# Attention layer of a decoder trunk: projection pieces ahead of the sparse products, one piece divided round the compressed scores, stick-breaking sums and scores interleaved

## The chip, the cores and the metric

One core of one Trainium2 chip runs the whole program. The metric is the device time of one execution in microseconds; lower is better. Of the before kernel three executions were timed, and one further execution was profiled. All times of rows below are from that profiled execution, in microseconds from the start of its span unless marked ns.

## What is computed

A trunk of two layers over 256 rows of width 1024, in float32. Layer 0 has the mixer that the change touches, layer 1 a gated recurrence; each is followed by a mixture of 32 experts of which a row uses two. The expert weights are read from memory once each.

```python
h = x
for layer in range(2):
    hn = rms_norm(h, norm_mix[layer])
    mix = nsa_stickbreak_mixer(hn, ...) if layer % 2 == 0 else hgrn2_mixer(hn, ...)
    h = h + mix
    h = h + hier_moe(rms_norm(h, norm_ffn[layer]), ...)
return rms_norm(h, final_norm)

# nsa_stickbreak_mixer
q_a, k_c, v_c, k_s, v_s, k_w, v_w, gate, q_b, k_b, v_b = split(h @ w_in)
o_cmp, sel_idx, sel_ok = nsa_compressed_and_select(q_a, compress(k_c), compress(v_c))   # 15 compressed blocks
o_sel, o_win = nsa_selected_and_window(q_a, k_s, v_s, k_w, v_w, sel_idx, sel_ok)        # softmax per branch
o_a = gate[0] * o_cmp + gate[1] * o_sel + gate[2] * o_win                              # 8 heads
# stick breaking, 8 heads
z = q_b @ k_b.T * scale
log_keep = where(before, log_sigmoid(-z), 0)
later = cumsum(log_keep, reverse=True) - log_keep
o_b = where(before, exp(log_sigmoid(z) + later), 0) @ v_b
return concatenate([o_a, o_b]) @ w_out
```

## The kernel before, in words

Five engines run instruction streams of their own, in the order in which the code writes them, and wait for each other by counting semaphores. Where an instruction waits, all that is behind it on its engine waits too. The change is in layer 0's attention, and there in TensorE's, ScalarE's and VectorE's order.

**Projections.** h @ w_in is computed in 12 parts, proj(0) to proj(11), each with 8 input blocks of 128 and two halves. A product is kept near float32 by splitting both operands into a high and a low part and adding three products: high by high and high by low in one run of 16 matmuls of 128x256 (L1770 with L1774 or L1772), then low by high in 8 more (L1781 or L1779). So one half of a part, called a piece here, is 24 matmuls. ScalarE makes the high part of a weight quarter (L798), VectorE the low part (L379). The parts alternate between banks 0 and 1; ScalarE empties the even parts (proj_even), VectorE the odd ones (proj_odd), and the semaphore proj_psum counts finished parts. proj(6) and proj(7) make the stick-breaking queries, proj(8) and proj(9) the keys, proj(10) and proj(11) the values.

**Compressed branch.** TensorE multiplies the compressed keys (L1872) and values (L1874), ScalarE copies them out (L920 to L922), and then 16 small matmuls with 15 columns each (L1888, two records each in the trace) make the compressed scores. VectorE masks them, takes the maxima and subtracts (L1280 to L1285), and ScalarE takes the exponentials (L930). The first sparse scores wait for that VectorE work (semaphore cmp_step). In the before kernel the whole of proj(6) stands behind the scores.

**Sparse branches.** Eight units, u = 0 to 7, are two query tiles by two branches (selected, window) by two halves of the heads. For each unit: scores on TensorE (nsa_scores, L1902), mask and maximum on VectorE (mask, L1298, L1301), exponentials on ScalarE (exps, L941), division and gate on VectorE (scale, L1308 to L1314), transposes of the probabilities on TensorE (nsa_T, L1914), copies out of the transposes on ScalarE (L973) and, for u of 4 and more, also on VectorE (L1355), and the product with the values on TensorE (nsa_pv, L1928). In turn u TensorE issues nsa_scores(u+1), nsa_pv(u-1), the pieces of a projection that a table PROJ_AT gives to this turn (one piece in turns 0 to 3, two in turns 4 to 6, none in turn 7), and nsa_T(u). Behind a finished odd part it raises unit_used (free_units), which lets the queue on SyncE load expert weights into the place of the weights just used. Turn 7 has the stick-breaking scores sb_z(0) and sb_z(1) ahead of nsa_T(7).

**Stick breaking.** Eight heads in four pairs. sb_z(pair) makes the scores of two heads and adds the mask (L1947, L1951, L1955). VectorE turns them into a maximum and a negative absolute value (sb_abs, L1323, L1324), ScalarE takes exponential and logarithm (exp_ln, L947, L948), VectorE adds the two (L1370, semaphore sb_t), TensorE adds the running sums to the scores in the same bank (sb_e, L1962 to L1964), ScalarE takes the exponential (L988, semaphore sb_a), and TensorE multiplies with the values (sb_pv, L1977). VectorE's third buffer makes sb_abs(hd) wait for sb_e(hd-3). Heads 6 and 7 use the banks of heads 0 and 1, so sb_z(3) waits for the first two exponentials of L988. Between them the result of the sparse branches is split too: ScalarE copies two banks (L983, mix_hi) and VectorE subtracts (out_low, L1359, mix_lo); sb_pv(0) and sb_pv(2) write into these banks and wait for it. Behind it all come the products with w_out (mix_front, mix_tile).

**Queue.** SyncE issues the weight loads in a fixed order, each behind a wait: at L418 for places in the ring, at L469 for the expert weights that go where the attention's buffers were. The last of these in the attention wait for sb_pv of all heads (L1977).

## Time and profile before

| | us |
|---|---|
| three timed executions | 743.26, 746.83, 748.84 (median 746.83) |
| profiled execution, its own time | 749.39 |
| its span, first to last instruction | 747.70 |
| mean granted TensorE clock | 0.938 of full speed |
| TensorE busy | 628.5 (84% of the span) |
| VectorE busy | 307.7 (41%) |
| ScalarE busy | 242.3 (32%) |

The page gives the chain of work that ended last as 52% TensorE and 32% DMA, and within the DMA share 30% is one kind of transfer, the experts' down weights. The busy shares are means over stages that are limited by different things, so they are read by stage: the first part of the span is layer 0's attention, then come routing and the first experts of layer 0, then a long stretch with the later experts; layer 1 has its recurrence in the place of the attention and the same experts' stages behind it. 1.69 us of the execution's time lie outside the span.

### The profile page before, as it was taken

The page shows a single profiled execution, that of the slowest core. Times are in us where ns is not written, and L with a number is a line of the kernel's source. Part 1 is how long each engine was busy: PE and PEld are TensorE (multiplying, and loading weights), DVE is VectorE, ACT ScalarE, POOL GpSimd, SP SyncE. Part 2 cuts the span into 40 slices and gives each one's busy share as a digit, 9 for nine tenths or more (in the row PEclk, how much of TensorE's full clock was granted, in tenths as well). Part 3 has the DMA queues.
Part 4 walks back from the last instruction along what each step waited for, and adds up shares of the span by engine and source line. Part 5 has one row for each costly group of instructions (what it writes and reads, how often), then busy time and mean ns, then how long its engine had stood idle before and what let it go on. Part 6 is the DMA issues. An engine that isn't in the chain of part 4 may idle for free.

```text
span 747.7 us, 11876 instructions
## 1 busy us (share of the span) xinstructions
PE 628.5 (84%) x4862; PEld 435.3 (58%) x4862; DVE 307.7 (41%) x536; ACT 242.3 (32%) x546; POOL 35.9 (5%) x64
## 2 busy tenths in 40 slices
PE   7999898799998674955989999999999984595775
PEld 6987687697444322413259999999854441331321
DVE  4555677645223211202276786754432220211204
ACT  5434544525121100101156675553521110110113
POOL 5100000000001100000000001060000000000000
PEclk9998999999999977979999999999999998887979
DMA  8967333699999999999997536369989999999993
GB/s 314 257 208 286 113 113 120 250 391 343 391 406 404 403 423 420 419 421 423 411 387 273 204 135 226 124 243 369 389 341 399 414 422 422 423 420 419 422 418 146
DMA packets 59857, 245.08 MB, mean 328 GB/s; under 512 B 4560, under 2 KB 8928, under 8 KB 39072
## 3 DMA queue, kind: packets, MB, share of 16 engines
q1 hardware_dynamic: 58400, 242.33, 82.9%
q0 software_dynamic: 768, 1.40, 0.6%
q8 instruction: 34, 0.56, 0.3%
q10 hardware_dynamic: 640, 0.67, 0.3%
q14 instruction: 15, 0.12, 0.0%
HBM read 243.34 MB, written 1.05 MB: 327 GB/s over the span
## 4 chain that ended last, share of the span: by engine, by line
PE 52%; DMA 32%; DVE 5%; SPq 5%; ACT 3%; issue 2%; DVEq 0%; ACTq 0%
DMA ring<-in_moe_w_down 30%; PE psum L1770 9%; PE psum L2184 6%; PE psum L2129 6%; PE psum L1779 5%; PE psum L1772 5%; PE psum L1781 4%; PE psum L1774 4%; SPq L510 3%; PE psum L2122 3%; SPq L477 2%; DMA ring<-in_att_w_in 2%; PE psum L2113 1%; PE psum L1928 1%; PE psum L2301 1%
## 5 line engine op out<-in xcount | busy, mean ns | idle before, releaser
L2129 PE MATMUL psum<-ring,xT 128*32 128x512 f32 x512 | 66.8, 678 | 35.4 <-DMA ring<-in_moe_w_up 35.4
L1501 DVE TENSOR_TENSOR arena<-psum,arena 128x256 f32<-128x256 f32 x16 | 6.8, 425 | 214.8 <-ACT arena L1016 214.8
L2129 PE MATMUL psum<-arena,xT 128*32 128x512 f32 x512 | 65.3, 668 | 35.5 <-DMA arena<-in_moe_w_up 35.5
L1012 ACT ACTIVATE arena<-psum 128x256 f32<-128x256 f32 x16 | 6.1, 384 | 206.1 <-PE psum L2129 206.1
L2184 PE MATMUL psum<-ring,arena 128*32 128x512 f32 x456 | 58.6, 595 | 12.6 <-DMA ring<-in_moe_w_down 12.6
L1770 PE MATMUL psum<-x_hi,w_hi 128*128 128x256 f32 x248 | 63.7, 293 | 1.5 <-DVE x_hi L1188 1.2
L798 ACT ACTIVATE w_hi<-ring 128x1024 fp32r<-128x1024 f32 x48 | 48.8, 1051 | 44.2 <-PE psum L1781 21.0
L2129 PEld LDWEIGHTS psum<-arena,xT 128*32 128x32 f32 x512 | 17.0, 121 | 79.0 <-issue 42.5
L2122 PE MATMUL psum<-arena,xg 128*128 128x128 f32 x512 | 61.8, 278 | 0.8 <-DVE arena L1487 0.8
L2129 PEld LDWEIGHTS psum<-ring,xT 128*32 128x32 f32 x512 | 16.9, 123 | 77.8 <-issue 41.1
L2122 PEld LDWEIGHTS psum<-arena,xg 128*128 128x128 f32 x512 | 59.6, 194 | 2.7 <-issue 2.7
L379 DVE TENSOR_TENSOR w_lo<-ring,w_hi 128x1024 fp32r<-128x1024 f32 x44 | 52.3, 1221 | 18.4 <-ACT w_hi L798 18.4
L2113 PE MATMUL psum<-xT,arena 128*128 128x512 f32 x128 | 57.7, 594 | 0.0
L1770 PEld LDWEIGHTS psum<-x_hi,w_hi 128*128 128x128 f32 x248 | 48.9, 197 | 3.2 <-issue 1.6
L1774 PE MATMUL psum<-x_hi,w_lo 128*128 128x256 f32 x192 | 48.5, 289 | 0.0
L1483 DVE TENSOR_TENSOR h<-psum,h 128x512 f32<-128x512 f32 x64 | 44.2, 690 | 9.3 <-PE psum L2113 8.2
L2184 PEld LDWEIGHTS psum<-ring,arena 128*32 128x32 f32 x456 | 15.0, 109 | 48.8 <-issue 33.2
L1770 PE MATMUL psum<-w_hi,x_hi 128*128 128x256 f32 x160 | 39.7, 286 | 0.9 <-issue 0.8
L1772 PE MATMUL psum<-w_lo,x_hi 128*128 128x256 f32 x160 | 39.2, 283 | 0.0
L1774 PEld LDWEIGHTS psum<-x_hi,w_lo 128*128 128x128 f32 x192 | 38.0, 198 | 0.0
L2113 PEld LDWEIGHTS psum<-xT,arena 128*128 128x128 f32 x128 | 23.1, 190 | 24.6 <-issue 24.6
L1781 PE MATMUL psum<-x_lo,w_hi 128*128 128x256 f32 x248 | 35.6, 287 | 0.1
(334 smaller groups left out, 1044.1 us busy)
## 6 DMA issues: line engine op xcount, KB each, us to landing
ring<-in_moe_w_down SPq DMA_DIRECT2D x54, 1024.0 KB, 20.7
ring<-in_moe_w_gate SPq DMA_DIRECT2D x32, 1024.0 KB, 15.7
ring<-in_moe_w_up SPq DMA_DIRECT2D x32, 1024.0 KB, 17.6
arena<-in_moe_w_gate SPq DMA_DIRECT2D x32, 1024.0 KB, 21.3
arena<-in_moe_w_up SPq DMA_DIRECT2D x32, 1024.0 KB, 23.2
ring<-in_rec_w_in SPq DMA_DIRECT2D x16, 1024.0 KB, 13.9
ring<-in_att_w_in SPq DMA_DIRECT2D x8, 1024.0 KB, 11.7
ring<-in_att_w_out SPq DMA_DIRECT2D x4, 1024.0 KB, 13.5
```

What stands on the lines that cost most here:

```text
L379: eng.tensor_tensor(quarter_lo(base, r), quarter(base, r), quarter_hi(r).bitcast(F32), ALU.subtract)\
L798: act.activation(quarter_hi(r), quarter(base, r), ACT.Copy).then_inc(s["w_high"], 1)
L1483: dve.tensor_tensor(v, bank(b), v, ALU.add).then_inc(done, 1)
L1770: pe.matmul(dst, a_hi(k), b_hi(k), start=(k == 0), stop=False)
L1772: pe.matmul(dst, a_hi(k), b_lo(k), start=False, stop=False)
L1774: pe.matmul(dst, a_lo(k), b_hi(k), start=False, stop=False)
L1779: last = pe.matmul(dst, a_lo(k), b_hi(k), start=False, stop=(k == KD - 1))
L1781: last = pe.matmul(dst, a_hi(k), b_lo(k), start=False, stop=(k == KD - 1))
L2113: pe.matmul(bank(b), shareT[:, t, :], y_rows[:, half * 512:(half + 1) * 512], start=True, stop=True).then_inc(s[f"combined{l}"], 1)
L2122: last = pe.matmul(gather_bank(k, first)[:, k % 4 * P:(k % 4 + 1) * P], xg_parts[:, t, k, :], slots[:, t].rearrange("p e c -> p (e c)"), s ...
L2129: return pe.matmul(bank(3)[e * CAP:(e + 1) * CAP, :].rearrange("p (w f) -> p w f", w=2), gatheredT[:, k, e * CAP:(e + 1) * CAP], w, start= ...
L2184: last = pe.matmul(bank(5 + c)[e * CAP:(e + 1) * CAP, :], hidT[:, j, e * CAP:(e + 1) * CAP], down_part(l, kind, e, j)[:, c * 512:(c + 1) * ...
```

## The change

It moves instructions and adds none. (1) proj(6) is cut into its two pieces; the first is issued ahead of the wait for the compressed keys and values, the second stays behind the compressed scores. (2) In every turn u the projection pieces and the raising of unit_used, and in turn 7 sb_z(0) and sb_z(1), are issued ahead of the product nsa_pv(u-1). (3) In stick breaking TensorE issues sb_e(0) ahead of sb_z(2) and sb_z(3) ahead of sb_e(3). (4) ScalarE copies the two sparse banks one at a time, behind the exponentials of heads 0 and 1, where it copied both ahead of the first; VectorE's two subtractions come with heads 2 and 4, where both came with head 1.

```diff
@@ scalar, stick breaking
             for hd in range(SB_H):
                 if hd + 2 < SB_H:
                     exp_ln(hd + 2)
-                if hd == 0:
-                    act.wait_ge(s["nsa_pv"], 8)
-                    for g in range(NSA_G):
-                        act.activation(mix_hi[:, 2 * g:2 * g + 2, :], bank(6 + g).rearrange("p (a t) -> p a t", a=2),
-                                       ACT.Copy).then_inc(s["oT_high"], 1)
                 act.wait_ge(s["sb_e"], hd + 1)
                 if hd >= 3:
                     act.wait_ge(s["sb_pv"], (hd - 3) // 2 * 2 + 2)
                 act.activation(za[:, hd % 3, :], bank(SB_BANKS[hd])[:, 0:384], ACT.Exp).then_inc(s["sb_a"], 1)
+                if hd < NSA_G:
+                    act.wait_ge(s["nsa_pv"], 8)
+                    act.activation(mix_hi[:, 2 * hd:2 * hd + 2, :], bank(6 + hd).rearrange("p (a t) -> p a t", a=2),
+                                   ACT.Copy).then_inc(s["oT_high"], 1)
@@ vector, stick breaking
                 if hd + 2 < SB_H:
                     sb_abs(hd + 2)
-                if hd == 1:
-                    for g in range(NSA_G):
-                        dve.wait_ge(s["oT_high"], g + 1)
-                        dve.wait_ge(s["proj_psum"], 12)
-                        out_low(2 * g, 6 + g)
+                if hd in (2, 4):
+                    g = hd // 2 - 1
+                    dve.wait_ge(s["oT_high"], g + 1)
+                    dve.wait_ge(s["proj_psum"], 12)
+                    out_low(2 * g, 6 + g)
@@ tensor, compressed branch
             last.then_inc(s["cmp_product"], 1)
+            proj(6, (0,))
             pe.wait_ge(s["cmp_kv_done"], 3)
             pe.wait_ge(s["proj_odd"], 1)
...
             last.then_inc(s["cmp_product"], 1)
-            proj(6)
+            proj(6, (1,))
@@ tensor, sparse branches
             for u in range(8):
                 if u + 1 < 8:
                     nsa_scores(u + 1)
+                if u in PROJ_AT:
+                    proj(*PROJ_AT[u])
+                if PROJ_DONE.get(u) in (7, 9, 11):
+                    free_units(1)
+                if u == 7:
+                    sb_z(0)
+                    sb_z(1)
                 if u == 1:
...
                 if u >= 1:
                     nsa_pv(u - 1)
-                if u in PROJ_AT:
-                    proj(*PROJ_AT[u])
-                if PROJ_DONE.get(u) in (7, 9, 11):
-                    free_units(1)
                 if u == 0:
...
                     last.then_inc(s["cmp_product"], 1)
-                if u == 7:
-                    sb_z(0)
-                    sb_z(1)
                 nsa_T(u)
@@ tensor, stick breaking
+            sb_e(0)
             sb_z(2)
-            sb_e(0)
             sb_e(1)
             sb_e(2)
+            sb_z(3)
             sb_e(3)
             sb_pv(0)
-            sb_z(3)
             sb_e(4)
```

The changed code is one line shorter above TensorE's part, so that L1770 of the rows before is L1769 in the changed kernel, L1774 is L1773, L1781 is L1780, and on ScalarE L988 becomes L983 and L983 becomes L986.

**First place: TensorE round the compressed scores.** Before, the small products of keys and values (L1872, L1874) are followed at once by the scores (L1888), and then by the first matmuls of proj(6):

```order
L1872 MATMUL psum<-arena 64x30 [waits cmp_step]
L1874 MATMUL psum<-arena 128x64 x2
L1888 MATMUL psum<-arena 128x15 [waits proj_odd,cmp_kv_done]
L1888 MATMUL psum<-arena 128x15 x15
L1770 MATMUL psum<-x_hi,w_hi 128x256 [waits w_low_dve,proj_even]
L1774 MATMUL psum<-x_hi,w_lo 128x256
```

Changed, here is the end of the first piece of proj(6), the scores, and the start of the second piece:

```order
L1773 MATMUL psum<-x_hi,w_lo 128x256
L1780 MATMUL psum<-x_lo,w_hi 128x256 x8
L1888 MATMUL psum<-arena 128x15 [waits proj_odd,cmp_kv_done]
L1888 MATMUL psum<-arena 128x15 x15
L1769 MATMUL psum<-x_hi,w_hi 128x256 [waits w_low_dve]
L1773 MATMUL psum<-x_hi,w_lo 128x256
```

The 24 matmuls of one piece have moved from behind the scores to ahead of them, and with them the wait for proj_even.

**Second place: TensorE in turn 4 of the sparse branches.** Before, between the transposes of unit 3 (first two rows) and proj(9) stand the scores of unit 5 and the product of unit 3 (L1928), with its wait for the copies out of the transposes:

```order
L1914 MATMUL psum<-ident,arena 128x128 [waits nsa_pT_even,nsa_scaled]
L1914 MATMUL psum<-ident,arena 128x128 x3
L1902 MATMUL psum<-arena 128x256 [waits nsa_masked]
L1902 MATMUL psum<-arena 128x256 x3
L1928 MATMUL psum<-arena 64x128 [waits nsa_pT_even]
L1928 MATMUL psum<-arena 64x128 x3
```

Changed, that product comes behind the last 8 matmuls of proj(9), directly ahead of the transposes of unit 4:

```order
L1780 MATMUL psum<-x_lo,w_hi 128x256 x8
L1928 MATMUL psum<-arena 64x128 [waits nsa_pT_even]
L1928 MATMUL psum<-arena 64x128 x3
L1914 MATMUL psum<-ident,arena 128x128 [waits nsa_pT_even,nsa_scaled]
L1914 MATMUL psum<-ident,arena 128x128 x7
L1902 MATMUL psum<-arena 128x256 [waits nsa_masked]
L1902 MATMUL psum<-arena 128x256 x3
```

The product has moved past two pieces, 48 matmuls; in turns 1 to 3 it is one piece, in turns 5 and 6 two, in turn 7 the four heads' scores.

**Third place: stick breaking, TensorE behind nsa_pv(7).** Before, sb_z(2) (L1947 to L1955) and then the sums sb_e(0):

```order
L1947 MATMUL psum<-arena 128x256 [waits nsa_pT_odd,nsa_pT_even]
L1947 MATMUL psum<-arena 128x256
L1951 MATMUL psum<-arena 128x128 x2
L1955 MATMUL psum<-before_r,ident_r 128x2x128 [waits sb_z_raw] x2
L1962 MATMUL psum<-arena 128x256 [waits sb_t]
L1963 MATMUL psum<-arena 128x128
L1964 MATMUL psum<-arena 128x128
```

Changed, the sums of the first head, then the same scores, then the sums of the second head:

```order
L1962 MATMUL psum<-arena 128x256 [waits sb_t]
L1963 MATMUL psum<-arena 128x128
L1964 MATMUL psum<-arena 128x128
L1947 MATMUL psum<-arena 128x256 [waits nsa_pT_odd,nsa_pT_even]
L1947 MATMUL psum<-arena 128x256
L1951 MATMUL psum<-arena 128x128 x2
L1955 MATMUL psum<-before_r,ident_r 128x2x128 [waits sb_z_raw] x2
L1962 MATMUL psum<-arena 128x256 [waits sb_t]
```

The scores of heads 4 and 5 have moved past one head's sums. On VectorE, before, the two subtractions L1359 stand between sb_abs(3) and the addition for head 2:

```order
L1323 TENSOR_SCALAR arena<-psum 128x384 [waits sb_e,sb_z]
L1324 SCALAR_TENSOR_TENSOR arena<-arena,psum 128x384 [waits dve_chain]
L1359 TENSOR_TENSOR mix_lo<-psum,mix_hi 128x512 [waits proj_psum,oT_high] x2
L1370 TENSOR_TENSOR arena<-arena 128x384 [waits sb_ln]
```

Changed, from sb_abs(3) on, with the first subtraction only behind sb_abs(4):

```order
L1322 TENSOR_SCALAR arena<-psum 128x384 [waits sb_e,sb_z]
L1323 SCALAR_TENSOR_TENSOR arena<-arena,psum 128x384 [waits dve_chain]
L1369 TENSOR_TENSOR arena<-arena 128x384 [waits sb_ln]
L1322 TENSOR_SCALAR arena<-psum 128x384 [waits sb_e,sb_z]
L1323 SCALAR_TENSOR_TENSOR arena<-arena,psum 128x384 [waits dve_chain]
L1358 TENSOR_TENSOR mix_lo<-psum,mix_hi 128x512 [waits proj_psum,oT_high]
L1369 TENSOR_TENSOR arena<-arena 128x384 [waits sb_ln]
```

The addition for head 2, and with it the sums sb_e(2), no longer stand behind the subtractions.

## Rows read from the trace of the kernel before

**Rows 1.** Windows: length, busy of each engine, granted clock, DMA share, GB/s.
```profile
120.00:130.00 10.00, 7.85 (x77) 6.27 (x78) 8.68 (x15) 3.89 (x8) 0.00 (x0) 1.00 0.63 214
130.00:149.00 19.00, 15.11 (x110) 12.19 (x111) 11.30 (x21) 11.56 (x23) 0.00 (x0) 1.00 0.60 247
...
226.00:375.00 149.00, 106.64 (x732) 46.02 (x728) 30.98 (x54) 18.85 (x52) 5.86 (x9) 0.87 1.01 415
...
144.00:146.00 2.00, 2.00 (x18) 1.83 (x18) 0.55 (x2) 0.22 (x1) 0.00 (x0) 1.00 0.00 0
```

**Rows 2.** Waits of the DMA queue on SyncE, 0 to 200 us: total, times, longest.
```profile
SPq L418 <- PEq L1838: 85.2, 5, 21.3
SPq L469 <- PE psum L1977: 16.8, 1, 16.8
```

**Rows 3.** Timeline of TensorE round the compressed scores: start, us, what, [idle before <-releaser].
```profile
53.62 2.48 PE L1888 MATMUL psum<-arena 64*128 64x15 f32 x32 [0.77 <-ACT arena L922]
56.03 0.58 PE L1770 MATMUL psum<-x_hi,w_hi 128*128 128x256 f32 x1
...
64.44 0.71 PE L1902 MATMUL psum<-arena 64*128 64x128 f32 x8
...
66.60 0.39 PE L1770 MATMUL psum<-x_hi,w_hi 128*128 128x256 f32 x1
...
69.57 0.60 PE L2007 MATMUL psum<-ident,arena 128*128 128x128 f32 x4
```

**Rows 4.** Windows of L1888 alone: length, PE busy, PEld busy, clock, DMA share, GB/s.
```profile
53.60:54.80 1.20, 1.19 (x22) 1.19 (x22) 1.00 0.95 323
54.87:56.10 1.23, 1.23 (x14) 1.12 (x12) 0.50 1.05 406
```

**Rows 5.** Timeline of VectorE, last work on the compressed scores ahead of cmp_step.
```profile
57.66 0.41 DVE L1285 TENSOR_TENSOR arena<-arena 128x240 f32<-128x240 f32 x1
```

**Rows 6.** Timeline of TensorE in turns 2 to 7, transposes L1914 and products L1928.
```profile
84.41 0.66 PE L1914 MATMUL psum<-ident,arena 128*128 128x128 f32 x4
...
90.85 0.66 PE L1914 MATMUL psum<-ident,arena 128*128 128x128 f32 x4 [1.07 <-DVE arena L1314]
...
93.67 0.66 PE L1928 MATMUL psum<-arena 128*64 128x128 f32 x8 [1.10 <-ACT arena L973]
...
100.54 1.06 PE L1914 MATMUL psum<-ident,arena 128*128 128x128 f32 x8 [0.26 <-issue]
...
102.86 1.09 PE L1928 MATMUL psum<-arena 128*64 128x128 f32 x16 [0.19 <-ACT arena L973]
...
112.97 1.09 PE L1928 MATMUL psum<-arena 128*64 128x128 f32 x16 [1.13 <-ACT arena L973]
...
120.25 1.06 PE L1914 MATMUL psum<-ident,arena 128*128 128x128 f32 x8 [0.26 <-issue]
...
122.19 1.09 PE L1928 MATMUL psum<-arena 128*64 128x128 f32 x16 [0.87 <-DVE arena L1355]
```

**Rows 7.** Timeline of VectorE, the scaling L1314 of units 2 and 4.
```profile
83.66 0.69 DVE L1314 TENSOR_TENSOR arena<-arena 128x512 f32<-128x512 f32 x1
...
97.69 1.23 DVE L1314 TENSOR_TENSOR arena<-arena 128x1024 f32<-128x1024 f32 x1
```

**Rows 8.** Timeline of TensorE in stick breaking: nsa_pv(7), sb_e(2), the last sb_pv.
```profile
127.85 1.09 PE L1928 MATMUL psum<-arena 128*64 128x128 f32 x16 [0.87 <-DVE arena L1355]
...
134.21 0.70 PE L1962 MATMUL psum<-arena 128*128 128x256 f32 x2 [2.10 <-DVE arena L1370]
...
147.46 0.87 PE L1977 MATMUL psum<-arena 128*64 128x256 f32 x8 [0.65 <-ACT arena L988]
```

**Rows 9.** Timeline of VectorE in stick breaking: sb_abs(3), subtractions, sb_abs(6).
```profile
131.34 0.56 DVE L1323 TENSOR_SCALAR arena<-psum 128x384 f32<-128x384 f32 x1 [1.65 <-PE psum L1964]
...
132.41 1.28 DVE L1359 TENSOR_TENSOR mix_lo<-psum,mix_hi 128x512 fp32r<-128x512 f32 x2
...
139.00 0.56 DVE L1323 TENSOR_SCALAR arena<-psum 128x384 f32<-128x384 f32 x1 [1.80 <-PE psum L1955]
```

## The prediction, made before the changed kernel ran

> **What bounds the kernel now.** I read the windows first, to see which stage is limited by what. From 226 to 375 us the DMA share is 1.01 at 415 GB/s: there the expert weights' arrival sets the pace [rows 1]. One could conclude that work on attention is worth nothing. The reader should look at two more things. From 144 to 146 us, at the end of attention, the DMA moved nothing at all [rows 1]. And the waits of the DMA queue name their releasers: 85.2 us in five waits for TensorE to free ring places, and 16.8 us for the last stick-breaking product [rows 2]. So the queue's stream of expert weights starts anew from an event in attention, and the weights that set the pace later are issued behind it. Whatever attention saves up to the last sb_pv, the whole rest of the program saves, DMA stage included. That is the exchange rate I use: 1 us for 1 us.
>
> Then I read TensorE's timeline through attention. It has three kinds of loss: a stretch at half clock round the compressed scores [rows 3, 4], waits ahead of the sparse products and transposes [rows 6], and waits in stick breaking [rows 8]. The change aims at all three, and each has another answer.
>
> **Part 1, the divided piece.** The scores start at 53.62 after a wait of 0.77, so TensorE is free at 52.85 [rows 3]. Three amounts can be won.
>
> First the wait: the piece fills it, 0.77.
>
> Second, the scores themselves. In the trace the clock falls inside them, from 2.4 to 1.2 GHz, at about 54.8, after TensorE had done little: small products, the wait, and matmuls of 15 columns. Before the fall 22 records take 1.20 us, 55 ns each; after it 14 take 1.23 [rows 4]. All 32 at the full clock take 32 x 0.055 = 1.75 us against 2.48: 0.73.
>
> Third, proj(6). Its two pieces last from 56.03 to 64.44, 8.41 us [rows 3]. A piece at the full clock, the one from 66.60 to 69.57, takes 2.97 [rows 3]; two take 5.94. So 2.47 are lost to the clock. Beside this the Trainium skill, page "TensorE: Matmul & The Clock Gate", section "Back-to-back issue gap", gives N / 2.4 + 2.5 ns for a matmul of N columns, 109 ns here. By it a piece would take 2.6 us and the loss would be 3.2; the row, 124 ns a matmul, decides.
>
> Whether the second and third amount come back depends on the clock. In the changed order a dense piece stands directly ahead of the scores, the quiet stretch shrinks from 3.25 us (52.85 to 56.10) to 1.75, and dense work follows. In 130 to 149 us TensorE is idle for 3.9 of 19 us, once for 2.10 at a stretch, and the clock stays at full speed [rows 1, 8]. I take the likelier case: no fall. Bounds are 0.77 (everything as slow as before) and 3.97.
>
> What is late now: the scores end at 52.85 + 2.97 + 1.75 = 57.57, that is 1.47 later than before. VectorE's softmax work ended 1.97 after the scores' end (57.66 + 0.41 against 56.10) [rows 3, 5], so it ends at 59.54. The second piece ends at 60.54. nsa_scores(0), which waits for that work, has 1.0 us of cover. The first sparse scores start at 60.5 instead of 64.44. **Gain 3.97.**
>
> **Part 2, pieces ahead of the sparse products.** Each nsa_pv that waited for ScalarE's or VectorE's copies now finds them done, because 3 to 6 us of projection stand ahead. But a wait that goes matters only where the following transposes are not held by VectorE. So I go through the turns.
>
> Turns 2 and 3: the transposes at 84.41 follow VectorE's scaling, which ends at 83.66 + 0.69 = 84.35 [rows 6, 7], and those at 90.85 waited 1.07 for it [rows 6]. The chain there is transposes, scores, mask, low parts of weights, scaling, transposes; TensorE's product is not in it. The changed order leaves that chain as it is, and TensorE waits at L1914 for what it did not wait at L1928. Nothing, bounds 0 and 1.
>
> Turn 4: the wait of 1.10 at 93.67 goes. VectorE's scaling ended at 97.69 + 1.23 = 98.92, the transposes came at 100.54 [rows 6, 7]: 1.62 of slack, more than 1.10. Turn 5: 0.19 at 102.86 goes, turn 6: 1.13 at 112.97 [rows 6]; they have the same two pieces and the same VectorE work, so the same slack. Sum 1.10 + 0.19 + 1.13 = 2.42, and I take it whole, since the three turns are alike.
>
> Turn 7: the wait of 0.87 at 122.19 goes too [rows 6], but from the transposes of unit 6 (120.25) on, VectorE sets the pace: it copies, makes a low part, scales and goes on with sb_abs(0) and sb_abs(1) without a pause (VectorE is busy 8.68 of 10 us [rows 1]). Its last copy of transposes comes behind these, and nsa_pv(7) waits for it. Nothing. **Gain 2.4**, bounds 1.1 and 3.3.
>
> The moved steps that others hang on: free_units now comes ahead of the product, so expert weights are issued up to 1 us earlier relative to the turn; the DMA share of 0.60 leaves room [rows 1].
>
> **Part 3, stick breaking.** From nsa_pv(7) at 127.85 to the last sb_pv at 147.46 it lasts 19.6 us [rows 8] for eight heads. VectorE has three operations of 0.56 per head (13.4 us in all) and is idle in two long waits: 1.65 for sb_e(0), which stood behind sb_z(2), and 1.80 for sb_z(3), which stood behind sb_e(3) and sb_pv(0) [rows 9]. Both orders are turned round. TensorE's wait of 2.10 at 134.21 [rows 8] is the first of these together with the subtractions of 1.28 us that stood ahead of the addition for head 2 [rows 9]. The subtractions stay in VectorE's total, so moving them wins nothing by itself; it lets ScalarE and TensorE start. If both waits went entirely, 3.45 would be won. New ones come: sb_e(1) now stands behind sb_z(2), and sb_abs(4) waits for it; sb_e(3) stands behind sb_z(3), which waits for ScalarE's exponential of head 1, and behind that sit sb_pv(0), ScalarE's head 3 and VectorE's sb_abs(6). From the lengths in the rows I put the first at 0.6 and the second, covered by sb_e(2), at nothing. **Gain 2.85**, bounds 1.3 (half of it becomes another wait) and 3.45.
>
> **Sum.** 3.97 + 2.42 + 2.85 = 9.24. The profiled execution would be 749.39 - 9.2 = 740.2. It lies 2.6 above the median of the timed runs; the same saving from the median of 746.83 gives **737.6 us**, 1.2% less. From no change a measurement of this kernel can tell about 1%, 7.5 us.
>
> **Rivals.**
>
> *The clock falls all the same.* Matmuls of 15 columns were what TensorE did when it fell, and they are still there in one block. If both pieces run as slowly as before, the first part wins 0.77 only, and the sum is 0.77 + 2.42 + 2.85 = 6.0: 740.8 us. For it: the fall came inside these very matmuls [rows 4]. Against: dense work is now on both sides of them. Chance 0.13.
>
> *The waits only change their place.* In turns 4 to 6 VectorE turns out to hold the transposes, and in stick breaking the new orders make as long waits as the old. Then part 1 stays and part 3 wins its lower bound: 4.0 + 0 + 1.3 = 5.3, 741.5 us. For it: turns 2 and 3 are of this kind already [rows 6, 7]. Against: 1.62 us of slack in turn 4. Chance 0.12.
>
> *The DMA stage takes the gain back.* If the later weights did not shift with attention, nothing would be seen: 746.8 us. Against: the empty DMA at 144 to 146 and the queue's named waits [rows 1, 2]. Chance 0.06.
>
> *Slower: half clock in stick breaking.* With its filler moved away, TensorE waits behind nsa_T(7) for VectorE's last copy, about 1.5 us, and then has small matmuls and short waits only. If that lowers the clock, the 15.11 busy us of 130 to 149 [rows 1] become 30.2, which is 11.2 more than the stretch of 19, and part 3 is lost: +11.2 - 6.4 = +4.8, 751.6 us. It becomes slower than before once some 60% of the stretch runs at 1.2 GHz. For it: the clock has fallen after quiet work once in this stage. Against: the present stretch has longer idle times and keeps its clock [rows 1, 8]. Chance 0.04.
>
> **How the numbers follow.** The forecast has 0.65. Its own range comes from the bounds that I hold possible together, gain 7 to 10, with the spread of the timed runs (743.26 to 748.84) on top: 734.5 to 741. The first two rivals lie at 740.8 and 741.5; taking them in with half their spread gives 734 to 742.5, and outside are the last two rivals and the tails, under 0.2. Faster by over 1%, below 739.4: nine tenths of 0.65 and a quarter of the first rival, 0.63. Slower by over 1% is most of the slower rival, 0.04. The rest, 0.33, is within 1%.
>
> **What the profile after would show.** Right: L1888 without a wait and in under 2 us, the clock at full speed from 50 to 65 us, nsa_scores(0) near 60.5; no waits at L1928 in turns 4 to 6, and in turns 2 and 3 a wait of about 1 us at L1914; transposes of unit 6 near 113.9; the last sb_pv near 138.2 and the queue's L469 loads right behind it; the stage of 226 to 375 unchanged in length. Wrong: a clock of 0.50 anywhere from 54 to 64 or from 118 to 138; waits at L1914 in turns 4 to 6; VectorE idle for more than 1 us between sb_abs operations; a last sb_pv that is 9 us earlier while the end of layer 0 is not.

## The result, and the profile after

The changed kernel takes 738.74 us, the median of four executions (736.00 to 741.19); four of the kernel before, measured beside it, took 743.26 to 748.84 with a median of 747.27. The ratio is 0.9892, 95% interval 0.9862 to 0.9922: a gain of 8 us, between 5.8 and 10.3. The forecast was 737.6. The profiled execution of the changed kernel has a span of 739.5 against 747.70, 8.2 less.

TensorE's timeline of the changed kernel through attention (start, us, what, idle before and releaser), to be held against [rows 3, 6, 8]:

```profile
51.73 0.66 PE L1873 MATMUL psum<-arena 128*128 128x64 f32 x4
...
55.23 1.96 PE L1888 MATMUL psum<-arena 64*128 64x15 f32 x32
...
60.19 0.49 PE L1902 MATMUL psum<-arena 64*128 64x128 f32 x4
...
79.98 0.65 PE L1914 MATMUL psum<-ident,arena 128*128 128x128 f32 x4 [1.14 <-DVE arena L1313]
...
86.43 0.66 PE L1914 MATMUL psum<-ident,arena 128*128 128x128 f32 x4 [1.07 <-DVE arena L1313]
...
94.78 0.98 PE L1914 MATMUL psum<-ident,arena 128*128 128x128 f32 x7
...
113.23 0.98 PE L1914 MATMUL psum<-ident,arena 128*128 128x128 f32 x7
...
120.58 1.09 PE L1928 MATMUL psum<-arena 128*64 128x128 f32 x16 [1.40 <-DVE arena L1354]
...
137.82 0.87 PE L1977 MATMUL psum<-arena 128*64 128x256 f32 x8 [0.65 <-ACT arena L983]
```

And four rows of the kernel before that were not shown yet, the compressed values, nsa_pv(1) in turn 2, and the first two experts' products:

```profile
52.19 0.66 PE L1874 MATMUL psum<-arena 128*128 128x64 f32 x4
...
80.63 0.66 PE L1928 MATMUL psum<-arena 128*64 128x128 f32 x8 [1.01 <-ACT arena L973]
...
181.88 2.02 PE L2122 MATMUL psum<-arena,xg 128*128 128x128 f32 x16 [0.42 <-DVE arena L1487]
...
185.68 1.05 PE L2122 MATMUL psum<-arena,xg 128*128 128x128 f32 x7
```

The last sb_pv starts at 137.82 instead of 147.46, 9.64 earlier. But the compressed values already start 0.46 earlier (51.73 against 52.19), ahead of everything that was changed. So starts are not compared below, only distances. By them the attention won 9.18, in four pieces:

| from, to | before | after | won | forecast |
|---|---|---|---|---|
| compressed values, nsa_scores(0) | 12.25 | 8.46 | 3.79 | 3.97 |
| nsa_scores(0), transposes of unit 6 | 55.81 | 53.04 | 2.77 | 2.42 |
| transposes of unit 6, nsa_pv(7) | 7.60 | 7.35 | 0.25 | 0 |
| nsa_pv(7), last sb_pv | 19.61 | 17.24 | 2.37 | 2.85 |

VectorE in stick breaking has two waits left. sb_abs(3) waits 0.43 for sb_e(0), where it waited 1.65 [rows 9], and sb_abs(4) has a new wait of 0.68 for sb_e(1). The 1.80 ahead of sb_abs(6), for sb_z(3), is gone:

```profile
122.86 0.56 DVE L1322 TENSOR_SCALAR arena<-psum 128x384 f32<-128x384 f32 x1 [0.43 <-PE psum L1964]
...
125.15 0.56 DVE L1322 TENSOR_SCALAR arena<-psum 128x384 f32<-128x384 f32 x1 [0.68 <-PE psum L1964]
```

Windows of the changed kernel (columns as in [rows 1]): the compressed scores, stick breaking, the start of the experts, and the long stage with the later experts:

```profile
50.00:65.00 15.00, 14.08 (x135) 13.21 (x134) 10.00 (x26) 5.67 (x18) 0.00 (x0) 1.00 0.86 310
118.00:138.00 20.00, 17.13 (x134) 13.75 (x132) 14.99 (x29) 13.38 (x28) 0.00 (x0) 1.00 0.64 256
174.00:177.00 3.00, 3.00 (x17) 1.27 (x20) 1.22 (x8) 0.74 (x3) 0.00 (x0) 0.53 0.51 202
218.00:366.00 148.00, 109.17 (x728) 46.39 (x728) 30.98 (x54) 18.84 (x52) 5.88 (x9) 0.86 1.01 415
```

The clock stays at full speed in both places where a rival had it fall. But it reads 0.53 at 174 to 177, while the kernel before kept 1.00 at the same place of the program (184 to 187 there). What that cost stands in TensorE's rows there:

```profile
172.26 2.71 PE L2122 MATMUL psum<-arena,xg 128*128 128x128 f32 x16 [0.42 <-DVE arena L1486]
...
177.68 0.49 PE L2122 MATMUL psum<-arena,xg 128*128 128x128 f32 x2
```

From the last sb_pv to the first expert product it is 34.44 (before 34.42), to the second 39.86 (before 38.22): 1.64 more, of which 1.62 lie between the two products. So 1.6 us of the attention's gain was lost again behind it. Queue and stage then follow one for one: the loads L477 that were issued at 226.31 before are issued at 218.31, 8.00 earlier, which is 9.64 less 1.64. From these loads to the last product that combines the experts of layer 0 (L2113, at 377.50 before and at 369.58 now) it is 151.19 and 151.27, so the long stage kept its length, at a DMA share of 1.01 and 415 GB/s as before. The span ends 8.2 earlier.

### The profile page after: what moved, and what is told of

It is laid out like the page before. It is cut to its first block, busy times and chain, and to the rows that moved or that the text cites. A ratio compares the mean times of both kernels' runs of the same rounds, so it can differ in the third digit from the quotient of the medians.

```text
span 739.5 us, 11876 instructions
## 1 busy us (share of the span) xinstructions
PE 630.8 (85%) x4862; PEld 433.1 (59%) x4862; DVE 307.3 (42%) x536; ACT 242.3 (33%) x546; POOL 37.0 (5%) x64
## 4 chain that ended last, share of the span: by engine, by line
PE 53%; DMA 29%; SPq 7%; DVE 6%; issue 2%; ACT 2%; DVEq 0%; ACTq 0%
DMA ring<-in_moe_w_down 23%; PE psum L1769 9%; PE psum L2129 7%; PE psum L2184 6%; PE psum L1778 5%; PE psum L1771 5%; DMA ring<-in_moe_w_up 4%; PE psum L1780 4%; PE psum L1773 3%; SPq L510 3%; PE psum L2122 3%; SPq L469 2%; SPq L477 2%; DMA ring<-in_att_w_in 2%; PE psum L2113 1%
## 5 line engine op out<-in xcount | busy, mean ns | idle before, releaser
L2129 PE MATMUL psum<-ring,xT 128*32 128x512 f32 x512 | 68.6, 693 | 32.5 <-DMA ring<-in_moe_w_up 32.5
L2184 PE MATMUL psum<-ring,arena 128*32 128x512 f32 x456 | 62.8, 636 | 12.4 <-DMA ring<-in_moe_w_down 12.4
L1769 PE MATMUL psum<-x_hi,w_hi 128*128 128x256 f32 x248 | 61.9, 288 | 1.5 <-DVE x_hi L1187 1.2
L2113 PE MATMUL psum<-xT,arena 128*128 128x512 f32 x128 | 57.7, 594 | 0.0
L1769 PEld LDWEIGHTS psum<-x_hi,w_hi 128*128 128x128 f32 x248 | 47.3, 191 | 3.4 <-issue 1.6
L1773 PE MATMUL psum<-x_hi,w_lo 128*128 128x256 f32 x192 | 47.0, 283 | 0.0
L1769 PE MATMUL psum<-w_hi,x_hi 128*128 128x256 f32 x160 | 39.8, 286 | 0.9 <-issue 0.8
L2113 PEld LDWEIGHTS psum<-xT,arena 128*128 128x128 f32 x128 | 23.1, 190 | 24.6 <-issue 24.6
L1773 PEld LDWEIGHTS psum<-x_hi,w_lo 128*128 128x128 f32 x192 | 36.7, 191 | 0.0
L1780 PE MATMUL psum<-x_lo,w_hi 128*128 128x256 f32 x248 | 34.8, 283 | 0.1
```

The costliest lines, as they stand in the source:

```text
L1769: pe.matmul(dst, a_hi(k), b_hi(k), start=(k == 0), stop=False)
L1773: pe.matmul(dst, a_lo(k), b_hi(k), start=False, stop=False)
L1780: last = pe.matmul(dst, a_hi(k), b_lo(k), start=False, stop=(k == KD - 1))
L2113: pe.matmul(bank(b), shareT[:, t, :], y_rows[:, half * 512:(half + 1) * 512], start=True, stop=True).then_inc(s[f"combined{l}"], 1)
L2129: return pe.matmul(bank(3)[e * CAP:(e + 1) * CAP, :].rearrange("p (w f) -> p w f", w=2), gatheredT[:, k, e * CAP:(e + 1) * CAP], w, start= ...
L2184: last = pe.matmul(bank(5 + c)[e * CAP:(e + 1) * CAP, :], hidT[:, j, e * CAP:(e + 1) * CAP], down_part(l, kind, e, j)[:, c * 512:(c + 1) * ...
```

## Experiments: one part at a time

**Part 1 alone**, on the kernel before:

```diff
             last.then_inc(s["cmp_product"], 1)
+            proj(6, (0,))
             pe.wait_ge(s["cmp_kv_done"], 3)
...
-            proj(6)
+            proj(6, (1,))
```

> Only the division of proj(6) round the compressed scores. Theory: the dense piece ahead of the scores keeps the clock at full speed from 50 to 65 us, L1888 takes under 2.0 us without a wait, the first sparse scores start about 4.0 us earlier than before (60.5 instead of 64.44), and the last sb_pv too (near 143.5 instead of 147.46): time about 4 us less, 743.3. Rival, the clock falls all the same: the first sparse scores are only 0.8 us earlier, no difference that can be measured. Rival, the parts help only together (VectorE's later softmax is then in the way): the gain at the first sparse scores is gone by the last sb_pv.

742.88 us, ratio 0.9940 (0.9914 to 0.9967). TensorE's timeline of this kernel:

```profile
52.08 0.66 PE L1874 MATMUL psum<-arena 128*128 128x64 f32 x4
...
55.59 1.96 PE L1889 MATMUL psum<-arena 64*128 64x15 f32 x32
...
60.55 0.72 PE L1903 MATMUL psum<-arena 64*128 64x128 f32 x8
...
143.54 0.65 PE L1978 MATMUL psum<-arena 128*64 128x256 f32 x4 [0.65 <-ACT arena L988]
```

8.47 from the compressed values to nsa_scores(0), as in the changed kernel, at the full clock. All that it wins there, 3.78, is still there at the last sb_pv (143.54 against 147.46, less 0.11 of earlier start: 3.81).

**Part 2 alone**: the pieces, free_units, sb_z(0) and sb_z(1) ahead of nsa_pv(u-1), as in the diff of the change.

> Only the pieces (and in turn 7 the stick-breaking scores) ahead of the sparse products. Theory: from the first sparse scores (L1902 at 64.44) to the transposes of unit 6 it takes 2.4 us less than the 55.8 of before, all of it in turns 4 to 6; in turns 2 and 3 TensorE waits about 1.1 us at L1914 instead of at L1928; in turn 7 nothing is won. Time about 2.4 us less. Rival, the waits only change their place: the distance shrinks by less than 1 us, with waits at L1914 in turns 4 to 6 as well.

742.72 us, ratio 0.9954 (0.9926 to 0.9982). Its TensorE timeline has three things to read:

```profile
50.32 0.66 PE L1874 MATMUL psum<-arena 128*128 128x64 f32 x4
51.74 1.96 PE L1888 MATMUL psum<-arena 64*128 64x15 f32 x32 [0.77 <-ACT arena L922]
...
59.57 0.71 PE L1902 MATMUL psum<-arena 64*128 64x128 f32 x8
...
112.63 1.09 PE L1914 MATMUL psum<-ident,arena 128*128 128x128 f32 x8
...
126.33 0.70 PE L1962 MATMUL psum<-arena 128*128 128x256 f32 x2 [2.09 <-DVE arena L1370]
...
127.86 1.22 PE L1962 MATMUL psum<-arena 128*128 128x256 f32 x2 [0.28 <-DVE arena L1370]
```

First, 59.57 to 112.63 is 53.06, so part 2 wins 2.75, the same as in the changed kernel. Second, the compressed scores stand as in the kernel before, with the same wait of 0.77, and yet they take 1.96, not 2.48 [rows 3]: in this execution the clock did not fall there. From the compressed values to nsa_scores(0) it is 9.25. So the fall of [rows 4] is not in every execution, and it costs 12.25 - 9.25 = 3.00; without it the divided piece wins 9.25 - 8.46 = 0.79, little more than the wait. Third, the clock fell in stick breaking instead, behind the wait of 2.09: the same two matmuls of L1962 take 0.70 ahead of the fall and 1.22 in it. That is the slower rival's fall, at a far smaller price than the rival gave: from nsa_pv(7) (119.98) to the last sb_pv (140.87) it is 20.89, 1.3 more than the 19.61 of the kernel before, where the rival had 11.2. In this kernel the filler of turn 7 has moved as in the changed kernel, while stick breaking has its order of before.

**Parts 3 and 4 alone**: stick breaking changed, the rest as before.

> Only stick breaking (TensorE's order and the four operations of ScalarE and VectorE). Theory: from nsa_pv(7) to the last sb_pv it takes 16.8 to 17.3 us instead of 19.6, VectorE idles less than 0.8 us at a stretch in between; time 2.4 to 2.9 us less. Rival, half clock in stick breaking: a clock of 0.50 between 128 and 146 us and a stretch of over 19.6 us.

744.77 us, ratio 0.9964 (0.9937 to 0.9992). TensorE's timeline:

```profile
53.46 2.36 PE L1887 MATMUL psum<-arena 64*128 64x15 f32 x32 [0.77 <-ACT arena L922]
...
127.68 1.09 PE L1927 MATMUL psum<-arena 128*64 128x128 f32 x16 [0.88 <-DVE arena L1354]
...
144.94 0.76 PE L1976 MATMUL psum<-arena 128*64 128x256 f32 x6 [0.65 <-ACT arena L983]
```

From nsa_pv(7) to the last sb_pv it is 17.26, so 2.35 won. The fall at the compressed scores is there. The three traces give 3.78, 2.75 and 2.35, together 8.88: by the distances the parts add up to what they win together (3.79 + 2.77 + 2.37 = 8.93), and none feeds another. The times are too wide to say so: by the ratios the parts win 4.5, 3.4 and 2.7 us, each within about 2 us, together 10.6 against 8.

**Which half of stick breaking wins.** Two kernels divide it, both on the changed kernel. In the first, ScalarE's copies and VectorE's subtractions go back to their old places (the first two hunks of the change undone), and TensorE's new order stays; in the second TensorE's order goes back and the copies and subtractions stay moved:

```diff
             # second kernel, TensorE
-            sb_e(0)
             sb_z(2)
+            sb_e(0)
             sb_e(1)
             sb_e(2)
-            sb_z(3)
             sb_e(3)
             sb_pv(0)
+            sb_z(3)
```

> The changed kernel with TensorE's new order everywhere, but ScalarE's two copies of the sparse banks and VectorE's two subtractions as before the change: both copies ahead of the first exponential of stick breaking, both subtractions at head 1. Asked of the trace: the distance from nsa_pv(7) to the last sb_pv, 19.61 before and 17.24 in the changed kernel, 2.37 won. Theory A, the order of TensorE did it and moving copies and subtractions wins nothing by itself, as the prediction has it for the subtractions: about 17.3 to 17.8. Theory B, the 1.28 of subtractions and the copies that stood ahead of the first exponential were the true delay: 19 or more. If both are needed, since the addition for head 2 and the exponential of head 0 still stand behind them, about 18.5. The time of the program follows at one to one: 738.7 to 739.3 by A, 740 to 741 by B.

> The counterpart: the changed kernel with ScalarE's copies and VectorE's subtractions moved, but TensorE in stick breaking as before, sb_z(2) ahead of sb_e(0) and sb_z(3) behind sb_pv(0). Theory A, TensorE's order did it: VectorE's waits of 1.65 and 1.80 stay, each at its place, and the distance from nsa_pv(7) to the last sb_pv is 19 or more; the program takes 740.5 to 741. Theory B, copies and subtractions did it: 17.3 to 17.8 and 739. If both are needed, the two distances of this kernel and its counterpart each lie between, and their gains add up to less than 2.37.

739.34 us (ratio 0.9897, 0.9862 to 0.9932) and 739.99 us (0.9908, 0.9872 to 0.9944). The first kernel's TensorE timeline, nsa_pv(7) and the last sb_pv:

```profile
119.09 1.09 PE L1929 MATMUL psum<-arena 128*64 128x128 f32 x16 [1.40 <-DVE arena L1355]
...
136.23 0.87 PE L1978 MATMUL psum<-arena 128*64 128x256 f32 x8 [0.65 <-ACT arena L988]
```

The second kernel's, and then its VectorE timeline:

```profile
118.97 0.88 PE L1928 MATMUL psum<-arena 128*64 128x128 f32 x12 [1.40 <-DVE arena L1354]
...
138.56 0.65 PE L1977 MATMUL psum<-arena 128*64 128x256 f32 x4 [0.65 <-ACT arena L983]
```

```profile
122.45 0.56 DVE L1322 TENSOR_SCALAR arena<-psum 128x384 f32<-128x384 f32 x1 [1.65 <-PE psum L1964]
...
129.52 0.56 DVE L1322 TENSOR_SCALAR arena<-psum 128x384 f32<-128x384 f32 x1 [1.81 <-PE psum L1955]
```

17.14 and 19.59. TensorE's two exchanges alone win 2.47, more than the 2.37 of all the moves in stick breaking together; moving the copies and the subtractions wins 0.02 without the exchanges and costs 0.10 with them. The 0.10 is small but stands clear: seven kernels that have the exchanges and the moved copies and run the stretch at the full clock give 17.24 to 17.26. In the second kernel VectorE's waits are back, 1.65 and 1.81 against 1.65 and 1.80 before. Theory A holds in the traces. The two times differ by 0.65 only, with overlapping intervals, and would not have told the theories apart; of the two profiled executions the first has the fall behind routing that was worth 1.62 above, and the second has not.

## Experiments: the clock at the compressed scores

**Is it the wait?** The kernel before, with three matmuls of 128x128 on constant operands in the wait (their results are read by nobody), and no piece of a projection moved:

```diff
             last.then_inc(s["cmp_product"], 1)
+            keep_clock(3, 7)
             pe.wait_ge(s["cmp_kv_done"], 3)
```

> The kernel before with three dense matmuls of 128x128 between the products of compressed keys and values and the wait of 0.77 us, no other change: they fill the wait (0.71 us). It asks what made the clock fall. If it was the idle 0.77 us together with the small matmuls, the clock stays at full speed, L1888 takes 1.75 us and the first sparse scores start 3.2 us earlier (61.2), time 3.2 us less. If the small matmuls alone do it and a whole dense piece ahead of them is needed, the clock falls at the same place and the first sparse scores start at 64.4 as before, time the same.

745.41 us, ratio 0.9968 (0.9941 to 0.9995). TensorE's timeline:

```profile
50.53 0.66 PE L1874 MATMUL psum<-arena 128*128 128x64 f32 x4
51.02 0.89 PE L1742 MATMUL psum<-ident 128*128 128x128 f32 x6
51.95 2.00 PE L1889 MATMUL psum<-arena 64*128 64x15 f32 x32
...
61.26 0.71 PE L1903 MATMUL psum<-arena 64*128 64x128 f32 x8
```

The wait is filled, and the clock falls all the same, at 53.7, for 3.4 us instead of 6.8. It is 10.73 to nsa_scores(0), between 9.25 without a fall and 12.25 with the long one. The wait is thus not needed for a fall, and since part 2 alone had the wait and no fall, it is not enough for one either. Whether the filler made the fall shorter or rarer stays open. One trace doesn't tell, and the time lies between the two answers of the expectation: 2.4 us less than before by the ratio (0.4 to 4.4), where 3.2 stood for a clock that stays and nothing for one that falls as before.

**Is the division needed?** The changed kernel with both pieces ahead of the scores:

```diff
-            proj(6, (0,))
+            proj(6)
             pe.wait_ge(s["cmp_kv_done"], 3)
...
-            proj(6, (1,))
```

> The changed kernel with both pieces of proj(6) ahead of the compressed scores instead of one on each side. It asks whether the second piece is needed as cover for VectorE's softmax. Theory: the scores end 3 us later than in the changed kernel (about 60.1), VectorE's work ends 2 us after that, and nsa_scores(0), with nothing left ahead of it, waits for it: it starts 1.9 to 2.1 us later than in the changed kernel (about 62.2 instead of 60.19), with a wait shown; time about 2 us more. Rival: the clock falls in the scores with the wait behind them, and the loss is 3 to 4 us.

740.42 us, ratio 0.9892 (0.9833 to 0.9951). TensorE's timeline, and a window behind it:

```profile
56.40 1.96 PE L1888 MATMUL psum<-arena 64*128 64x15 f32 x32
60.40 1.23 PE L1901 MATMUL psum<-arena 64*128 64x128 f32 x8 [2.04 <-DVE arena L1284]
```

```profile
60.00:67.00 7.00, 5.81 (x32) 5.29 (x33) 5.40 (x14) 5.19 (x17) 0.00 (x0) 0.51 1.05 387
```

The second piece is what covers VectorE's softmax work: without it nsa_scores(0) waits 2.04, and in this execution the clock falls within this wait, at 60.1. The compressed values stand at 50.00 here and the last sb_pv at 139.72: 89.72 against 86.09 in the changed kernel, 3.63 more, of which 1.94 come ahead of nsa_scores(0) and the rest behind it at half clock. In size this is the rival's loss (3 to 4), though the clock fell in the wait and not in the scores, which take 1.96. The time of this run, 1.7 above the changed kernel's, can't be told from it.

## Experiments: what attention is worth behind it

The prediction took 1 us for 1 us, because the queue's stream starts anew behind the last sb_pv. Two kernels add the same 34 idle matmuls to the changed kernel, once ahead of the last sb_pv, so that the queue starts later, and once behind it, so that the queue starts as early as ever and only TensorE is late:

```diff
             # first kernel
             sb_pv(2)
+            keep_clock(34, 2)
             sb_pv(3)
             # second kernel
             sb_pv(3)
+            keep_clock(34, 2)
```

> The changed kernel with 34 added dense matmuls (8.0 us, their product is used by nothing) on TensorE ahead of the last sb_pv, so that both TensorE's further work and the start of the queue's next loads come 8.0 us later. It asks at what rate time in attention becomes time of the program. Theory, 1 for 1: the time is 8.0 us above the changed kernel's, about that of before, with every later stage shifted by 8.0. Rival, the later experts' stage, limited by the weights' arrival, absorbs part of it: less than 6 us.

> The same 34 matmuls directly behind the last sb_pv: TensorE's path is 8.0 us later, but the queue's four loads of expert weights that wait for sb_pv are not. If the weights' arrival sets the pace from attention's end on, their head start of 8 us makes the time rise by much less than 8.0; if TensorE's own path (output products, routing, first experts) sets it until the later experts' stage, and all the loads behind those four wait for TensorE again, it rises by the same 8.0. I expect 6 to 8.

745.45 us (743.08 to 747.98, ratio 0.9973) and 745.74 us (743.65 to 748.68, ratio 0.9985). The first kernel's TensorE timeline, and the second's:

```profile
135.52 7.86 PE L1741 MATMUL psum<-ident 128*128 128x128 f32 x68
143.31 0.87 PE L1977 MATMUL psum<-arena 128*64 128x256 f32 x8
...
177.75 2.02 PE L2123 MATMUL psum<-arena,xg 128*128 128x128 f32 x16 [0.42 <-DVE arena L1486]
```

```profile
136.62 0.87 PE L1977 MATMUL psum<-arena 128*64 128x256 f32 x8 [0.65 <-ACT arena L983]
137.43 7.75 PE L1741 MATMUL psum<-ident 128*128 128x128 f32 x67
...
178.47 1.80 PE L2123 MATMUL psum<-arena,xg 128*128 128x128 f32 x14 [0.42 <-DVE arena L1486]
```

The filler took 7.86 and 7.75 us but delayed TensorE by less. In the first kernel the distance from the compressed values (50.11) to the last sb_pv is 93.20 instead of 86.09, 7.1 more, since the filler also covers the wait of 0.65 there. In the second the distance from the last sb_pv to the first expert product is 41.85 instead of 34.44, 7.4 more. Against this, the two lost 6.7 and 7.0 us by the medians, 6.0 and 6.9 by the ratios (each of these is good to about 3 us only: the intervals of the ratios are 0.9944 to 1.0002 and 0.9955 to 1.0015, and the changed kernel has its own).

In the second kernel the queue's L469 loads went out at 137.54, 6.7 us ahead of the first's (144.22), and no gain from it is to be seen: the second lost no less than the first. The rate is near one for one, but not by the road that the prediction named. What carries the delay is TensorE's own path, through w_out and routing to the first experts. The loads behind those four wait for TensorE again: the next L477 goes out 23.05 behind the last sb_pv in the changed kernel and in the first one, and 30.45 behind it in the second (167.07), 7.4 later, and the next L469 there at 182.40, directly behind the second expert product at 182.27.

## Experiments: further than the change

**VectorE's scaling first.** In turns 2 and 3 the transposes still wait 1.14 and 1.07 for VectorE, as forecast. VectorE makes low parts of weights ahead of the scaling; this kernel turns the two round there:

```diff
+                if u in (2, 3):
+                    scale(u)
                 for r in LOW_AT.get(u, ()):
                     split_low(dve, U_QB, r, "att")
...
-                scale(u)
+                if u not in (2, 3):
+                    scale(u)
```

> The changed kernel with one more move: in turns 2 and 3 VectorE scales unit u before it makes the low parts of weights, so that the transposes do not wait for the low parts. It tests the reading that turns 2 and 3 gained nothing because VectorE's chain (mask, low parts, scaling) holds the transposes. Theory: the waits of 1.14 and 1.07 us at L1914 in turns 2 and 3 go, the low parts fall into VectorE's waits for the next scores, and the last sb_pv is 2.0 to 2.3 us earlier; time about 2.2 us less. Rival, ScalarE's exponentials hold the scaling as well: less than 1 us, and VectorE waits at L1307 for ScalarE.

735.40 us, ratio 0.9834 (0.9774 to 0.9894). TensorE's transposes of units 2 and 3 in this kernel:

```profile
77.02 0.66 PE L1917 MATMUL psum<-ident,arena 128*128 128x128 f32 x4
...
82.33 0.66 PE L1917 MATMUL psum<-ident,arena 128*128 128x128 f32 x4
```

Both waits are gone, and from nsa_scores(0) (58.44) to the transposes of unit 6 (109.14) it is 50.70 against 53.04: 2.34 more are won, as forecast. The time says more, 4.3 us by the ratios, but the two intervals overlap, and the traces show nothing in attention beyond the 2.34.

**The fall behind routing.** Small idle matmuls fill TensorE's two waits there, 0.71 and 0.42, in both layers:

```diff
-        START, FIRST, ROUTE, NORM = 16, 8, 19, 10
+        START, FIRST, ROUTE, NORM = 16, 8, 22, 10
...
                     .then_inc(s["total_psum"], 1)
+                keep_clock(2, 3)
```

> The changed kernel with small matmuls on constant operands added where TensorE waits in routing: 22 in place of 19 in the existing filler, and three more behind the count of members, in both layers; their results are read by nobody. Theory A: the half clock at 173.4 to 176.8 in the changed kernel's trace came from quiet work in routing, and this keeps the clock full; the last routing piece and the first experts behind it win up to 1.6, and the program up to 1.6 in executions that had the fall, nothing in others: 737 to 738.7. Rival B: the clock falls there by the accident of the execution, or falls a little later; the trace then shows a stretch at 0.50 between 165 and 185 all the same, and the time stays at 738.7. Rival C: the filler itself lengthens the path, 739 to 740.

> The kernel of scale_first (VectorE's scaling ahead of the low parts in turns 2 and 3, 735.4 in its run) with the filler of route_filled. If filling routing wins, this is the fastest kernel, 734 to 735. If the filler does nothing, it is 735.4 again within 1; if it lies on the path, 736 to 737. Either way it should be below the changed kernel's 738.7 by 2.3 or more, which is the distance won in attention in the trace of scale_first.

735.57 us (ratio 0.9860, 0.9826 to 0.9894), and with the scaling first 734.04 us (733.29 to 734.46, ratio 0.9829, 0.9804 to 0.9855). The first of the two, a window and the second expert product:

```profile
174.00:177.00 3.00, 3.00 (x32) 2.08 (x28) 0.34 (x1) 0.00 (x0) 0.00 (x0) 1.00 0.51 124
```

```profile
174.51 2.05 PE L2123 MATMUL psum<-arena,xg 128*128 128x128 f32 x16
```

That product stands 38.24 behind the last sb_pv (136.27), as before the change and 1.62 less than in the changed kernel; neither of the two traces has a fall in either layer's routing. The filler itself costs nothing (first expert product at 34.43). But this does not prove that the filler did it. Of the twelve profiled kernels without it, two have a fall between the first two expert products of layer 0, seven have one at the same place in layer 1 (5.4 us from product to product there instead of 3.8), and the others kept their clock. The times speak for the filler without settling it: 0.9860 against 0.9892, intervals overlapping, and 735.57 lies below the 737 that theory A allowed at best. The last kernel is the fastest of all, and its interval lies just below the changed kernel's.

## Why the prediction was right, and where it was off

**Part 1, 3.97 forecast, 3.79 measured.** Wait gone, second piece at full clock, VectorE's work covered by it. The scores took 1.89 up to the next start where 1.75 was put, since 55 ns each was too little (1.96 for 32 records, 61 ns), and the two pieces 3.03 and 3.07 where 2.97 was put. By starts alone, 0.96 was won ahead of the scores (0.77 forecast), 0.52 in them (0.73 forecast) and 2.31 in the two pieces (2.47 forecast). The forecast also counts 0.07 twice: it ends the scores at 56.10 and starts the pieces at 56.03 [rows 3], and its own start of nsa_scores(0), 60.54, is 3.90 below 64.44 and not 3.97. The Trainium skill ("TensorE: Matmul & The Clock Gate", "Back-to-back issue gap") gives N / 2.4 + 2.5 ns as the gap of an isolated matmul at the full clock, and says itself that streams with weight loads depart from it. By it a piece would take 2.6, an estimate; the changed kernel's 3.03 and 3.07 lie above it, as the row of 2.97 did. What the forecast did not know is that 3.00 of its gain exist only in executions in which the clock falls at the scores. Of the four kernels with the old order there, three profiled executions had the fall and one did not; of nine with the divided piece none had it. That the divided piece keeps the clock rests on this count; by which of its effects (the wait gone, dense work ahead or behind) it does so stays open. With the wait filled and no dense work ahead the clock still fell, and with both pieces ahead and none behind it fell in the wait that followed, in one execution each. Timed alone the part wins 4.5 us (2.5 to 6.4), more than the 0.79 that it has without a fall, which points to the fall being in most executions.

**Part 2, 2.42 forecast, 2.77 measured.** The three waits are gone, and turns 2 and 3 won nothing, as said: in turn 2 the 1.01 that nsa_pv(1) waited is now 1.14 at the transposes, and in turn 3 the transposes wait 1.07 as before. Turn 4 won 1.34 instead of 1.10: between the transposes of units 3 and 4 it was 9.69 and is 8.35, and the 0.26 marked as issue there [rows 6] is gone too. Turns 5 and 6 won 0.14 and 1.12, the way to unit 2's transposes 0.18. Turn 7, put at nothing, won 0.25: the wait ahead of nsa_pv(7) grew from 0.87 to 1.40, since VectorE sets the pace, as argued.

**Part 3, 2.85 forecast, 2.37 measured.** The new wait for sb_e(1) was put at 0.6 and is 0.68, the one for sb_z(3) at nothing and is nothing. Left out was that sb_abs(3) still waits 0.43 for sb_e(0). 3.45 - 0.43 - 0.68 = 2.34. That the subtractions win nothing by moving was right; that moving them "lets ScalarE and TensorE start" was not: they could have stayed. The prediction also read TensorE's wait of 2.10 as made partly by the subtractions; TensorE's order alone took the stretch to 17.14 with the subtractions where they were.

**The sum, 9.24 forecast, 9.18 measured** up to the last sb_pv. That the two lie within 0.06 is luck in part: parts 1 and 3 were put 0.18 and 0.48 too high, part 2 and turn 7 together 0.60 too low. The program then lost 1.6 to a clock fall in the first experts, which no rival had named, so the profiled executions differ by 8.2. The rate of one for one held, for another reason than given: not the queue's restart, TensorE's path.

**The rivals.** The clock did not fall at the scores. A wait only changed its place in turn 2, where it was forecast. The DMA stage took nothing back. The half clock in stick breaking is real, but was seen only with TensorE's old order there: in two of the five profiled kernels that have it, for 3.4 us each (part 2 alone, and the one with the filled wait), and in none of the nine with the new. That is too few to say that the new order prevents it. Each cost 1.3 to 1.5 us (20.89 and 21.07 from nsa_pv(7) to the last sb_pv).

## What to carry to other kernels

Read which work lies between a wait and the engine that set it: a dense piece put into a quiet stretch can pay twice, for the wait and, in the executions in which the clock would fall there, for the clock, and the piece has to be divided so that enough is left behind to cover the next engine's work. In a chain of small steps across engines, the order on the engine that many wait for decided here; where another engine's moved work was not what anybody waited for, leave it. And when two profiled executions are compared, subtract the clock falls first, place by place, and compare distances, not start times.

## What the runs showed of the hardware

The granted clock falls from 2.4 to 1.2 GHz for stretches of 3.4, 6.8 or 10.2 us in the traces (those of 10.2 only in the experts' stages). In attention and behind routing the falls come at a few places in the program, but not in every execution. The clearest case lies ahead of all that was edited, in the dense projections at 16 to 21 us. The changed kernel, and the kernel with the filled routing, same window:

```profile
16.00:21.00 5.00, 5.00 (x32) 5.00 (x31) 4.04 (x4) 2.23 (x3) 0.77 (x1) 0.66 1.04 385
```

```profile
16.00:21.00 5.00, 5.00 (x44) 5.00 (x43) 3.94 (x4) 2.12 (x3) 0.77 (x1) 1.00 1.03 382
```

TensorE is busy all the time in both windows, and the instructions up to there are the same. But directly ahead of them it was quiet: it had waited for ScalarE's high part of a weight, here in the kernel before:

```profile
15.98 1.19 PE L1788 MATMUL psum<-x_hi,w_hi 128*128 128x256 f32 x8 [2.10 <-ACT w_hi L895]
```

Four of the fourteen profiled executions had this fall (before, changed, part 1 alone, stick breaking alone), and in these the compressed values start at 51.7 to 52.2; in the others they start at 50.0 to 50.6. The same wait was 1.87 to 2.10 in the four with the fall. In the ten without it was 1.42 to 1.73 in eight, and 1.90 and 2.05 in two (TensorE's order alone, and the fastest kernel). So the falls came with the longer waits, but the length of the wait alone doesn't decide. Such falls, 1.6 us each here and behind routing, are of the size of the few us by which executions of one kernel differ; that they make up this difference was not shown, since each kernel has one profiled execution, and what decides whether the clock falls, these runs don't show.
